# First expert of an encoder layer: its token slots by counted comparisons, later weight loads, another order of its matmuls

## The reference, cut to what matters

```python
def expert_choice_ffn(h, w_router, w_exp_gate, w_exp_up, w_exp_down):
    tok = h.reshape(N, D)                         # N = 512 tokens of one group
    aff = softmax((tok @ w_router).astype(f32))   # 16 experts
    cap = EC_CAPACITY_FACTOR * N // N_EXPERTS     # 64 tokens for each expert
    gate, idx = lax.top_k(aff.T, cap)
    xs = tok[idx]
    hid = silu(xs @ w_exp_gate) * (xs @ w_exp_up) # 1024 -> 2048
    out = (hid @ w_exp_down) * gate[..., None]    # 2048 -> 1024
    y = zeros.at[idx].add(out)
```

## Time and profile before

| | us |
|---|---|
| median of three runs | 2387.05 |
| the profiled execution, its own time | 2386.68 |
| its span, first to last instruction | 2384.8 |
| TensorE matmul busy | 2360.4 |
| VectorE busy | 1624.6 |
| ScalarE busy | 1488.6 |
| GpSimd busy | 401.4 |

### The profile page before, as it was taken

One profiled execution on the slowest core, in us unless ns is written; L12 is line 12 of the kernel. 1 busy time (PEld: TensorE's weight loads), 2 busy tenths in 40 slices (PEclk: granted clock), 3 DMA queues, 4 the chain that ended last, 5 costly groups with the idle time before them and its releaser, 6 DMA issues.

```text
span 2384.8 us, 33778 instructions
## 1 busy us (share of the span) xinstructions
PE 2360.4 (99%) x11804; PEld 1967.3 (82%) x11804; DVE 1624.6 (68%) x1767; ACT 1488.6 (62%) x1707; POOL 401.4 (17%) x279
## 2 busy tenths in 40 slices
PE   8999999999999999999998999999999999999998
PEld 7888888888888888888885888888888888888886
DVE  5545464634546455455346988888888888888897
ACT  5656564533466465554335777777777777777776
POOL 1533433000053324320002000000000000000000
PEclk9999999999999999999999999999999999999999
DMA  6413321125432224112238999999999999999998
GB/s 189 128 45 100 88 73 67 70 98 204 158 98 83 83 62 126 64 63 80 90 155 334 403 393 382 383 383 381 390 387 393 387 383 383 385 387 376 394 375 326
DMA packets 214395, 557.35 MB, mean 234 GB/s; under 512 B 11968, under 2 KB 93376, under 8 KB 209216
## 3 DMA queue, kind: packets, MB, share of 16 engines
q1 hardware_dynamic: 207280, 530.89, 60.4%
q0 software_dynamic: 7056, 25.69, 3.6%
HBM read 533.47 MB, written 23.07 MB: 233 GB/s over the span
## 4 chain that ended last, share of the span: by engine, by line
PE 97%; DVE 1%; DMA 0%; issue 0%; ACT 0%; POOLq 0%; SPq 0%; DVEq 0%; ACTq 0%
PE bank L1433 44%; PE bank L1073 15%; PE bank L1118 13%; PE bank L1039 7%; PE bank L1062 5%; PE bank L1093 3%; PE bank L1236 2%; PE bank L1479 2%; PE bank L1134 2%; PE bank L1217 1%; PE bank L1156 1%; PE bank L1197 1%; PE bank L1203 1%; PE bank L1160 1%; PE bank L1252 0%
## 5 line engine op out<-in xcount | busy, mean ns | idle before, releaser
L2575 DVE TENSOR_TENSOR m_lo<-m_raw,m_hi 128x2048 fp32r<-128x2048 f32 x380 | 867.4, 2290 | 121.0 <-ACT m_hi L1925 117.4
L1925 ACT ACTIVATE m_hi<-m_raw 128x2048 fp32r<-128x2048 f32 x382 | 733.6, 1921 | 261.5 <-PE bank L1433 256.6
L1433 PE MATMUL bank<-m_hi,xs_hi 128*128 128x512 f32 x1032 | 321.0, 392 | 0.0
L1433 PE MATMUL bank<-m_hi,xs_lo 128*128 128x512 f32 x1032 | 317.9, 389 | 0.0
L1433 PE MATMUL bank<-m_lo,xs_hi 128*128 128x512 f32 x1032 | 317.8, 389 | 0.0
L2063 DVE TENSOR_TENSOR w_lo<-w_raw,w_hi 128x1152 fp32r<-128x1152 f32 (+4 forms) x110 | 145.0, 1344 | 180.1 <-ACT w_hi L1561 180.0
L1433 PEld LDWEIGHTS bank<-m_lo,xs_hi 128*128 128x128 f32 x1032 | 193.7, 188 | 40.5
L1433 PEld LDWEIGHTS bank<-m_hi,xs_lo 128*128 128x128 f32 x1032 | 193.7, 188 | 40.4
L1433 PEld LDWEIGHTS bank<-m_hi,xs_hi 128*128 128x128 f32 x1032 | 191.4, 188 | 38.2 <-DVE xs_lo L2597 0.2
L1073 PE MATMUL bank<-h_hi,w_hi 128*128 128x512 f32 x512 | 203.0, 396 | 0.0
L1073 PE MATMUL bank<-h_lo,w_hi 128*128 128x512 f32 x512 | 199.6, 390 | 0.0
(11 more groups left out here) (292 smaller groups left out, 4239.4 us busy)
## 6 DMA issues: line engine op xcount, KB each, us to landing
m_raw<-in_w_exp_gate SPq DMA_DIRECT2D x128, 1024.0 KB, 8.1
m_raw<-in_w_exp_up SPq DMA_DIRECT2D x128, 1024.0 KB, 7.6
m_raw<-in_w_exp_down SPq DMA_DIRECT2D x128, 1024.0 KB, 7.4
w_raw<-in_w_b SPq DMA_DIRECT2D x66, 512.0 KB, 6.2
w_raw<-in_w_a SPq DMA_DIRECT2D x24, 1024.0 KB, 5.1
w_raw<-in_w_c SPq DMA_DIRECT2D x24, 1024.0 KB, 4.8
w_raw<-in_w_d SPq DMA_DIRECT2D x8, 1024.0 KB, 6.5
xt<-in_x SPq DMA_DIRECT2D x8, 512.0 KB, 7.9
```

Of the source, the lines that this page charges most:

```text
L1433: mm = pe.matmul(ps[:, half, :], a[:, chunk + k, :], v[:, k, 512 * half:512 * (half + 1)], start=first and k == n == 0, stop=last and k == ...
L1925: act.activation(m_hi[slot.slot][:, :, :], m_raw[raw.slot][:, :, :], ACT.Copy)\
L2575: dve.tensor_tensor(m_lo[slot.slot][:, :, :], m_raw[raw.slot][:, :, :], m_hi[slot.slot][:, :, :].bitcast(F32), ALU.subtract)\
```

## The change

- The first expert's 64 slots of each group no longer come from the 8 rounds. The affinities of expert 0 are laid on all partitions by transposes (t); VectorE compares each token of a tile with all tokens of this tile and those before it (r: one instruction for ties, one for "greater" with a row sum); TensorE counts the columns (c, bfloat16); VectorE marks which token has which rank (o); TensorE picks row number and gate by small matmuls (q); VectorE copies them out (p). For group 0 this lies inside the last D stage, for group 1 after the softmax.
- The 8 rounds, the merge and the lists of the other 15 experts move behind that, in between VectorE's splits of the first expert's units. The idle matmuls beside the rounds go.
- GpSimd no longer splits units 0 and 1, but 0, 5 and 10, each told to start when VectorE starts rounds.
- SyncE loads units 0 and 1 at once, waits ahead of unit 2 for the stores of `normed`, and ahead of unit 4 until the first gather has landed (before: only unit 7 waited). final_gain is loaded later. A table of 0.4 MB is loaded in the D stage.
- Expert 0 runs gate 0, up 0, gate 1, up 1, down 0, down 1, and then gate 0 and up 0 of expert 1; the loop covers 14 experts and not 15.

```diff
-WARM_START, WARM_FIRST, WARM_GATHER, WARM_SPLIT, WARM_NORM = 3, 1, 6, 2, 4
-WARM_ROUNDS = {1: 1, 2: 1, 3: 1, 4: 1, 5: 1, 6: 1, 7: 1}
+WARM_START, WARM_FIRST, WARM_GATHER, WARM_SPLIT, WARM_NORM = 3, 1, 4, 2, 4
+POOLED = (0, 5, 10)
@@ closing_schedule(last)
+        if last and i == NT - 2:
+            out += [("t", 0, i) for i in range(NT)]
+    if last:
+        out += [("r", 0, j) for j in range(NT + 1)]
+    out += [("D", 1, 0), *((("c", 0), ("o", 0)) if last else ()), ("Y", 0), ...
...
-                ("E", 2), ("E", 3), ("e", 2), ("b", 0), ("e", 3), ("B", 3)]
+                ("t", 1, 1), ("E", 2), ("E", 3), ("e", 2), ("t", 1, 2), ("e", 3), ("t", 1, 3), ("q", 0), ("b", 0),
+                ("Z", 1), ("r", 1, 0), ("r", 1, 1), ("r", 1, 2), ("r", 1, 3), ("r", 1, 4), ("c", 1), ("o", 1), ("q", 1), ("p", 1),
+                ("B", 3)]
@@ sync, load_expert_unit
-                if unit.k == RAW_SLOTS - 1:
+                if unit.k == 2:
+                    for each in s_store_n:
+                        sp.wait_ge(each, 16 * NB)
+                if unit.k == 4:
                     sp.wait_ge(s_gather, 16)
+                    sp.wait_ge(s_picked, 2 * NB)
@@ gpsimd
+            for n, k in enumerate(POOLED):
+                pool.wait_ge(s_mhi, k + 1)
+                pool.wait_ge(s_rounds, n + 1)
+                pool.tensor_tensor(m_lo[cut][:, :, :], m_raw[raw][:, :, :], ...).then_inc(s_plo, 1)
+            pool.wait_ge(s_route, 2)
             ...
             gather(1, 1)
@@ tensor
+                elif what == "t":
+                    pe.wait_ge(s_aff, of * NT + i + 1)
+                    pe.transpose(ranked[of][:, natural(i)], aff[:, i, 0:1].to_broadcast([P, P]), ident[:, :])
+                elif what == "c":
+                    for j in range(NT - 1, 0, -1):
+                        pe.wait_ge(s_beats, i * NT + NT - j)
+                        for k in range(j):
+                            last = pe.matmul(counts[i], beats[j][:, natural(k)], unit_cols[:, k, :], ...)
+                elif what == "q":
+                    8 matmuls (hot_16 x tokens_16, 1 column), then 4 (hot x first_aff, 1 column)
             token_transposes(16)
             keep_busy(WARM_SPLIT, ps_proj[:, 0, :])
             operand_ready(1)
             gate_cols(True)
             up_cols()
+            gate_cols()
+            hidden_transposes(1)
+            up_cols(True)
+            down(0, 0, hid_hi, hid_lo)
+            token_transposes(32)
+            hidden_transposes(2)
+            down(0, 1, hid_hi, hid_lo)
+            operand_ready()
+            gate_cols()
+            up_cols()
@@ scalar: the same order; behind unit 11:
+            split 12-15, swish_step, hid_hi, split 16-23, xs_hi, hid_hi, split 24-27, output_scaled(0), split 28-31, swish_step, split 32-35
@@ vector
+            dve.scalar_tensor_tensor(tie[j][:, 0:cols], ranked[of][:, 0:cols], aff[:, j, 0:1], later[...], is_equal, mult)
+            dve.scalar_tensor_tensor(beats[j][:, :], ranked[of][:, 0:cols], aff[:, j, 0:1], tie[j][...], is_gt, add, accum_out=row_sum[...])
...
+            rounds 0 to 2, xs_lo, split 1-3, split 4, rounds 3 to 5 (GpSimd: unit 5), split 6-9,
+            round 6 (GpSimd: unit 10), hidden_step, round 7, split 11, 12, halves_merged, split 13, hid_lo,
+            split 14, routes, split 15, split 16-19, hidden_step, split 20-23, xs_lo, hid_lo, split 24-33, hidden_step, split 34, 35
```

More of the change, by code:

```diff
@@ L602, in tile_read, with lo_ready @@
             eng.wait_ge(s_proj_free[proj.slot], START + proj.lap + 1)
+        def lo_ready(eng, unit, behind=0):
+            k = unit.k - behind
+            if k in POOLED:
+                eng.wait_ge(s_plo, POOLED.index(k) + 1)
+            else:
+                eng.wait_ge(s_mlo, unit.n(1 - behind - sum(each < k for each in POOLED)))
         def all_stored(eng, count):
@@ L2038, in _ @@
             split_units()
+            after()
+            split_units()
+            swish_step()
+            transposed_hi(hid_hi)
+            after()
+            split_units()
+            after()
+            split_units()
+            transposed_hi(xs_hi)
+            transposed_hi(hid_hi)
+            after()
+            split_units()
+            output_scaled(0)
+            after()
+            split_units()
+            swish_step()
+            after()
+            split_units()
             per = {"raw": 24, "slot": 24, "unit": 24, "done": 24, "tr": 6, "step": 2}
-            with rolled(act, NE - 1, mt, per) as e:
-                expert(e)
+            with rolled(act, NE - 2, mt, per) as e:
+                expert(e + 1)
             last_expert()
@@ L2540, in _ @@
                 then(ins)
[L2541 to L2550, removed]
@@ L2677, in last_expert, with split_unless_pooled @@
                                          ALU.mult, ALU.mult).then_inc(s_rowout, 1)
[L2681 to L2685 removed]
+            def split_unless_pooled():
+                if unit.k in POOLED:
+                    for x in (raw, slot, unit):
+                        x.k += 1
+                else:
+                    split_units(1)
+            dve.sem_inc(s_rounds, 1)
+            eight_best(0)
+            eight_best(1)
+            eight_best(2)
+            split_unless_pooled()
+            transposed_lo(xs_hi, xs_lo)
+            split_units(3)
+            after()
+            split_units(1)
+            split_unless_pooled()
+            dve.sem_inc(s_rounds, 1)
+            eight_best(3)
+            eight_best(4)
+            eight_best(5)
+            split_units(2)
+            after()
+            split_units(2)
+            split_unless_pooled()
+            dve.sem_inc(s_rounds, 1)
+            eight_best(6)
+            hidden_step()
+            eight_best(7)
+            split_units(1)
+            after()
+            split_units(1)
+            halves_merged()
+            split_units(1)
+            transposed_lo(hid_hi, hid_lo)
+            split_units(1)
+            routes()
+            split_units(1)
+            after()
+            split_units()
+            hidden_step()
+            after()
+            split_units()
             transposed_lo(xs_hi, xs_lo)
[L2687 removed]
+            transposed_lo(hid_hi, hid_lo)
             after()
```

231 lines of the change are left out of this document (168 added, 63 removed), and 1 row of the table out.

## The result

The changed kernel takes 2394.47 us (median of 8 runs, 2392.89 to 2396.19) against 2387.73 for the kernel before beside it (2385.47 to 2388.45): ratio 1.0032, 95% interval 1.0022 to 1.0041. It is slower by some 7 us, 0.3%. 2389.5 was predicted, with a range to 2393.5 and "no change" as the likeliest sign; both were missed. The profiled execution took 2392.89, the lowest of the eight; its span is 2391.1 (before: 2384.8).

A forecast was written before the change was run, and what follows sets the result against it. TensorE, busy for 99% of the span, was taken as the bound. Choice -8.2, group 0 +0.9, first expert +0.9, turn +6.9 and clock +2.3 sum to +2.8 us on 2386.68: 2389.5 us, range 2381.5 to 2393.5.

The forecast's parts named there:

- no change: Whole kernel: time between 2382.3 and 2391.8 us, too near the kernel before to tell apart; chance 0.56.
- Part 1, the choice: Seam, first expert's choice by counting: 6.7 us in place of 14.90, 8.2 us less (6.1 to 9.3).
- the rest of the route stays: Seam behind the choice: unchanged at 0.99 us to GpSimd, 5.05 for the gather, 2.21 on TensorE.
- part 5: Loads of the first expert's units: the new waits cost nothing, with 0.7 us in hand at unit 4.
- Part 2: Group 0's choice inside the D stage, where TensorE has no idle time: 0.9 us more (0.6 to 1.8).
- Part 3: VectorE's rounds and splits through the first expert: late splits of units 14 and 15 cost 0.9 us (0 to 3).
- Part 4, the turn: Between units 19 and 20: TensorE waits for the hidden tile turned through ScalarE and VectorE, 6.9 us lost.
- The clock: Stop at unit 20 and about 4 us beyond: TensorE at 1.2 GHz, 2.3 us lost (0 to 3).
- the fourth rival: First expert: rounds lock GpSimd out, splits take 7 us, units 5 and 10 come 2.5 late; 2394.5 us, chance 0.07.
- The third rival: First expert: held loads starve it from about unit 11, costing 4.0 us by unit 20; 2393.5 us, chance 0.12.

The follow-up runs named there:

- e2: The changed kernel without the wait for the stores of normed ahead of unit 2; 2389.81 us.
- e4: The changed kernel with GpSimd's split of unit 0 held until the first gather has landed; 2395.71 us.
- e8: e7 with units 4 to 6 asked for at once too, only unit 7 waiting for the gather; 2388.96 us.
- e1: The changed kernel with expert 0's second half in the old order, loads and other engines to match; 2387.33 us.
- e5: The changed kernel with idle matmuls in the turn, four calls between the two groups of transposes and one behind them; 2392.44 us.
- e6: The changed kernel, new order kept, but the next tokens transposed after the second unit of down 0; 2393.95 us.
- e11: e7 with VectorE waiting for its own last split to end before it tells GpSimd to start units 5 and 10; 2382.27 us.
- e7: The changed kernel with the changes of e1 and e2 together; 2382.28 us, ratio 0.9979 to the kernel before.
- e10: e7 with VectorE splitting units 5 and 10 itself and GpSimd only unit 0; 2384.39 us.
- e9: The kernel before with units 4 to 6 held until the first gather has landed; 2386.87 us, ratio 1.0002.

## Why the prediction was wrong

- *Part 1, the choice:* right in mechanism. 6.7 us were forecast, 6.0 measured; the nine instructions took 3.9 us (1264.73 to 1268.60), not 3.4, and the hand-overs and small matmuls the rest, 1.6 and not 2.7. The price from below (no cost of the row sum) was the right one; what was too dear were the hand-overs, whose size no row had shown.
- *Part 1, "the rest of the route stays", and part 5, "the wait ahead of unit 2 holds nothing that is needed before S":* **the step that failed.** The prediction took the gather at its old 5.05 us, with no bound above. The wait held units 2 and 3 until the stores were down, at 1268.9, and so put 2 MB on the DMA engines right ahead of the gather of 1271.14, which then took 8.10. I asked whether the units would be late for TensorE, and not what they would meet. e2 brings the gather back to 4.9 us, e4 rules the GpSimd split out, e8 brings it to 8.4 us with other loads. The five executions with the hold agree in the order too: where the last held load was asked for 1.3 to 1.4 us ahead of the gather it took 8.1 us (the changed kernel, e4), where it was 0.2 to 0.5 us it took 9.1 to 9.5 (e1, e5, e6). Price: 3.05 us for the gather and 0.44 for ScalarE's late split of unit 3, less the 0.5 by which the stores were quicker; e2's first pair ends 2.9 us earlier, and the runs differ by 3.5 to 4.7. Why the median lies 1.6 us above the profiled execution is open. e1, e5 and e6 show what such runs may hold: with the rows later still, the idle matmuls in front of the first unit and this unit's first matmuls ran at half clock. How often that happened in the unprofiled runs can't be seen.
- *Part 2:* 0.9 forecast. The counts took TensorE 0.30 us for six, and VectorE was in time (beats at 1236.6, counts read at 1237.84). The last affinity is 0.56 us later than before (1264.15 against 1263.59). Somewhat under. In the nine experiments that contain this part it lies between 1263.60 and 1264.93, so a single execution gives it to half a microsecond at best.
- *Part 3:* 0.9 forecast, 1.6 measured (0.35 and 1.3). The rule of the Trainium skill (SBUF — State Buffer, Who interferes with whom) bore on more places than the one that was reckoned. For unit 11 the forecast was a wait of 0.9 us behind GpSimd's unit 10, and VectorE's split took 3.23 us there where 2.29 is usual:

```profile
1308.23 3.23 DVE L2734 TENSOR_TENSOR m_lo<-m_raw,m_hi 128x2048 fp32r<-128x2048 f32 x1
```

Not reckoned were the starts of units 5 and 10. VectorE's signal runs ahead of its work: GpSimd began 1.05 us before VectorE's four splits ended (1290.42 against 1291.47, where VectorE's next instruction starts), and its split took 5.64 us, 1.1 more than the 4.54 of unit 0. At unit 10 it began 0.76 us early and took 0.79 more. By the rule the later one waits, and e11 agrees: 4.64 and 4.65 once they start behind it. But these waits are not what part 3 had too small, since e11 is no faster than e7. The forecast had its 0.9 as late splits of units 14 and 15, and of such waits only 0.19 us show, at unit 14; that the sum comes near is partly luck. The rest of the 1.3 us arises at units 12 to 14 too: 0.2 for the two transposes of the lists, which no term held, and units that take 2.94 us and more in place of 2.72, whose cause is open. As to the rounds the measurement agrees with what was read from the earlier trace rows, so the fourth rival is refuted. e10 shows that the margins of 0.1 us were not as sharp as I made them.
- *Part 4, the turn:* right, 6.9 forecast and 7.3 measured, by the order that was told (the unit first, then xs_lo, then the hidden tile), and undone by e1 (8.5 us with the clock, 9.6 but for the new wait of 1.1). The clock: 2.3 forecast, 2.3 measured behind the restart and 3.2 by e5 with what it costs in the turn.
- *Sum:* +2.8 forecast, +6.3 in the spans. The missing 3.5 us are the gather (3.05), the first pair behind the rows (0.44), part 3 (0.7) and the turn (0.4), less the 0.7 by which the choice was shorter than forecast and some 0.3 of part 2; that makes 3.6. A bound on the gather was to be had: the page of the kernel before has 8.1 us from issue to landing for the 1 MB loads of `in_w_exp_gate` beside their neighbours, where the earlier trace rows, the row that was used, has 4.8. Some 3 us for it at the upper end would have given 2396.5.
- *The third rival* (loads starve the first expert) is refuted: ScalarE did wait for units 4 and 5 (3.69 and 0.96 us, unit 4 being there 6.4 us after it was asked for and not 4.8), but TensorE's waits for `m_lo` stay at 0.2 us in the changed kernel.

## What to carry to other kernels

When a wait is put ahead of a transfer, ask what the transfer will meet when it is let go, not only whether it comes in time: two loads that were harmless early cost about 3 us when they were released just ahead of the small transfer on the critical path. When an operand is turned through other engines, keep matmuls between the turn and its first use (e6 shows that one such turn is enough for most of the stop), and read the cost from the longest queue of work that stands ahead of the turn on each of those engines. A choice that is 9 us faster pays only if both of these are kept; then it gave 4.3 us (e7). A further 1.1 us stand in e7 as TensorE's wait for the second gather.

## What the runs showed that I had not expected

- A gather of 128 rows took 4.5 to 5.2 us from its issue to TensorE's first use where no held loads came just ahead of it (the kernel before, e2, e7, e9, e10, e11), 8.1 to 9.5 with two 1 MB loads let go just ahead of it (the changed kernel, e1, e4, e5, e6), and 8.4 with the tail of seven (e8). In the first group the DMA engines had loads to move for at most about the first microsecond of it.
- A semaphore increment that stands by itself in VectorE's list was seen by GpSimd about 1 us before the instruction ahead of it had ended (1290.42 against 1291.47).
- The same idle matmuls left TensorE at 2.4 GHz for the rows of a gather of 5 us and still for those of 8.1 us in the changed kernel, which it had awaited for 3.05 us without work. With 8.4 us in e8 and 9.5 in e6 the transposes took 1.94 us and not 1.06, and in e1 the four idle matmuls behind the transposes took 3.42 us and not 1.88.
